# Where the early quarters of the first team's gate weights stand in SyncE's queue: between the attention loads or between the retention loads

## The reference, cut to what matters

```
h = rms_norm(x, g_mix)
proj = h @ w_in                      # q, k, v of 3 attention groups; retention q, k, v, g; two branch gates
outs, lses = per group (window, dilation): dilated_window_attention(q, k, v)       # 8 heads of 64
o_attn = sum over groups of softmax(lses) * outs
yr = retention_chunkwise(qr, kr, vr)                                               # 4 heads
o_ret = silu(gr_swish) * group_norm(yr)
merged = sigmoid(gate_a) * (o_attn @ w_attn_branch) + sigmoid(gate_r) * (o_ret @ w_ret_branch)
x = x + merged @ w_out
h2 = rms_norm(x, g_ffn)
y = hier_moe(h2, ...)                # 32 experts in 4 groups: top 1 group, top 2 experts inside it
out = rms_norm(x + y, g_final)
```

## Time and profile before

| | us |
|---|---|
| median of 3 runs | 804.96 |
| lowest, highest | 804.38, 806.15 |
| the profiled execution, its own time | 804.96 |
| its span | 803.2 |
| PE busy | 588.0 (73%) |
| DVE busy, ACT busy | 249.7, 196.9 |

### The profile page before, as it was taken

The page is one execution under the profiler, slowest core; times in us unless marked ns, Lnnn a source line. Parts: engine busy times, 40 slices in busy tenths (PEclk is TensorE's granted clock), DMA queues, the critical chain, the costliest instruction groups (busy, mean ns, idle before and its releaser), DMA issues.

```text
span 803.2 us, 11626 instructions
## 1 busy us (share of the span) xinstructions
PE 588.0 (73%) x4469; PEld 419.7 (52%) x4469; DVE 249.7 (31%) x432; ACT 196.9 (25%) x290; POOL 13.5 (2%) x28
## 2 busy tenths in 40 slices
PE   3999999999999999965690780780770870960966
PEld 3999999999999998852320320320320320320321
DVE  6776675866664455571000010010010010010001
ACT  5454554565555443330000000000000000000001
POOL 3000000000000000010000000000000000000000
PEclk9999999999999999988795795795895795895887
DMA  8758658255686555899999999999999999999991
GB/s 235 236 141 261 174 166 261 78 158 157 167 241 194 185 182 187 338 401 408 428 427 426 428 428 426 425 431 423 428 428 426 431 426 423 432 429 423 431 397 54
DMA packets 92758, 255.82 MB, mean 318 GB/s; under 512 B 8640, under 2 KB 70080, under 8 KB 80448
## 3 DMA queue, kind: packets, MB, share of 16 engines
q1 hardware_dynamic: 90512, 255.35, 82.9%
q10 hardware_dynamic: 2224, 0.17, 0.2%
HBM read 254.45 MB, written 1.05 MB: 318 GB/s over the span
## 4 chain that ended last, share of the span: by engine, by line
PE 65%; DMA 30%; DVE 2%; ACT 1%; issue 1%; POOL 0%; SPq 0%; DVEq 0%; ACTq 0%
PE ps L1032 64%; DMA ring<-in_w_down 27%; DMA ring<-in_w_up 2%; DMA gain<-in_g_mix 1%; ACT work L581 1%; DVE hn L706 1%; DVE work L887 0%; PE ps L1111 0%; POOL rstd L488 0%; PE ps L1135 0%; DVE hn L1026 0%; ACT work L673 0%; DVE hT L714 0%; DVE split L682 0%; DVE work L890 0%
## 5 line engine op out<-in xcount | busy, mean ns | idle before, releaser
L1032 PE MATMUL ps<-store,work 128*32 128x512 f32 x128 | 73.6, 740 | 182.2 <-DMA ring<-in_w_down 182.2
L1032 PE MATMUL ps<-ring,work 128*32 128x512 f32 x896 | 186.4, 614 | 1.6 <-DVE work L964 0.9
L682 DVE TENSOR_TENSOR split<-ring,split 128x768 fp32r<-128x768 f32 (+2 forms) x132 | 120.8, 932 | 92.4 <-ACT split L533 91.8
L1032 PE MATMUL ps<-hT,split 128*128 128x256 f32 x1152 | 141.9, 286 | 1.8 <-DVE hT L714 1.8
L1032 PEld LDWEIGHTS ps<-hT,split 128*128 128x128 f32 x1152 | 140.3, 194 | 2.8 <-issue 2.3
L1032 PEld LDWEIGHTS ps<-store,work 128*32 128x32 f32 x128 | 16.1, 132 | 232.1 <-DMA ring<-in_w_down 168.7
L533 ACT ACTIVATE split<-ring 128x768 fp32r<-128x768 f32 (+2 forms) x132 | 107.3, 825 | 120.2 <-PE ps L1032 101.6
L1032 PE MATMUL ps<-split,hT 128*128 128x256 f32 (+2 forms) x672 | 106.5, 316 | 0.0
L1032 PEld LDWEIGHTS ps<-split,hT 128*128 128x128 f32 x672 | 98.1, 190 | 4.4 <-issue 0.5
L964 DVE COPY work<-ps 128x512 f32<-128x512 f32 x8 | 5.5, 692 | 254.6 <-PE ps L1032 254.6
L1032 PE MATMUL ps<-hT_slot,work 128*32 128x512 f32 x128 | 73.6, 740 | 0.0
(11 more groups left out here) (176 smaller groups left out, 474.8 us busy)
## 6 DMA issues: line engine op xcount, KB each, us to landing
ring<-in_w_up SPq DMA_DIRECT2D x24, 2048.0 KB, 34.7
ring<-in_w_gate SPq DMA_DIRECT2D x18, 2048.0 KB, 24.9
ring<-in_w_in SPq DMA_DIRECT2D x96, 192.0 KB, 3.9
oRT_slot<-in_w_down SPq DMA_DIRECT2D x8, 2048.0 KB, 26.2
mid<-in_w_up SPq DMA_DIRECT2D x8, 2048.0 KB, 34.3
store<-in_w_down SPq DMA_DIRECT2D x8, 2048.0 KB, 17.4
hT_slot<-in_w_down SPq DMA_DIRECT2D x8, 2048.0 KB, 21.8
ring<-in_w_in SPq DMA_DIRECT2D x96, 128.0 KB, 2.4
```

Source lines behind the costliest of these rows:

```text
L682: dve.tensor_tensor(split[:, s, 1, 0:n], raw(s, n), split[:, s, 0, 0:n].bitcast(F32), ALU.subtract).then_inc(lo_ready, 1)
L1032: return pe.matmul(o, lhsT=l, rhs=r, start=start, stop=stop, skip_group_check=shared)
```

## The change

The sixteen quarters move from the attention loads to the retention loads. There are four retention iterations, as there were four attention iterations, so each iteration again takes quarter `i` of each of the four experts: one after the first quad, one after the second, two after the third. `load_pair` issues its three quads back to back. PE's wait for `early` names RET_HEADS in place of PAIRS, which is the same number. No other engine's stream changes.

```diff
-            def quarter(slot, src, i):
-                sp.dma_start(slots[slot][:, bass.ds(i * 1024, 1024)], src).then_inc(early, 16)
-
             def load_pair(i):
-                load_quad(3 * i, columns_of(attn_v[0], NG, P, i))
-                quarter(3, wg_v[0][:, bass.ds(i * 1024, 1024)], i)
-                load_quad(3 * i + 1, columns_of(attn_v[1], NG, P, i))
-                quarter(4, wg_v[1][:, bass.ds(i * 1024, 1024)], i)
-                load_quad(3 * i + 2, columns_of(attn_v[2], NG, P, i))
-                quarter(5, wg_v[2][:, bass.ds(i * 1024, 1024)], i)
-                quarter(10, wg_v[3][:, bass.ds(i * 1024, 1024)], i)
+                for m in range(3):
+                    load_quad(3 * i + m, columns_of(attn_v[m], NG, P, i))
 
             load_pair(0)
             with sp.Fori(1, PAIRS) as i:
                 load_pair(i)
 
+            def quarter(slot, src, i):
+                sp.dma_start(slots[slot][:, bass.ds(i * 1024, 1024)], src).then_inc(early, 16)
+
             with sp.Fori(0, RET_HEADS) as i:
                 load_quad(Q_RET + 3 * i, columns_of(qk_v, 2, RK, i))
+                quarter(3, wg_v[0][:, bass.ds(i * 1024, 1024)], i)
                 load_quad(Q_RET + 1 + 3 * i, plain_columns(COL_RV, RV, i))
+                quarter(4, wg_v[1][:, bass.ds(i * 1024, 1024)], i)
                 load_quad(Q_RET + 2 + 3 * i, plain_columns(COL_RG, RV, i))
+                quarter(5, wg_v[2][:, bass.ds(i * 1024, 1024)], i)
+                quarter(10, wg_v[3][:, bass.ds(i * 1024, 1024)], i)
...
-                    pe.wait_ge(early, 16 * TEAM * PAIRS)
+                    pe.wait_ge(early, 16 * TEAM * RET_HEADS)
```

## The result

| | kernel before | changed kernel |
|---|---|---|
| median of 6 runs, us | 804.57 | 810.79 |
| lowest to highest, us | 804.38 to 806.15 | 809.15 to 812.18 |
| ratio, 95% interval | | 1.0065, 1.0050 to 1.0081 |
| span of the profiled execution, us | 803.2 | 811.1 |

The median lies 2.8 us above the range. The ratio is that of the means, 810.09 us over 19 runs of the changed kernel (the table's six and thirteen more, 807.26 to 811.62 us) and 804.84 us over the six of the kernel before: 5.2 us. The two medians of the table are 6.2 us apart. Stretches of the changed kernel show where it went. The first row is an attention iteration, the next four are the retention iterations (each from PE's first matmul of one head to that of the next); the columns are those of the earlier trace rows.

What follows compares the result with a forecast made beforehand. PE's matmuls bound the kernel to 338.9 us, then the expert weights' DMA. Attention 0, retention 0 (0 to 0.2 at the dear end) and stream 0 left the time at 805.0 us, range 803.4 to 808.0.

Steps and rivals of the forecast that it cites:

- What bounds the kernel now: PE's own matmuls up to 338.9 us, then the expert weights' DMA; PE waits for no load in attention or retention.
- Attention gives nothing back: Attention stage: removing four 512 KB quarters an iteration gains 0, within bounds of 0 to 1.5 us.
- SP and throughput are not the bound: Retention iteration: SP busy 16.1 of 19.6 us; DMA 16.1 to 19.8 us, expected share 0.80 to 0.90.
- The first pair: Two quarters between quads 14 and 15 hold the queue up to 4.3 us; PE keeps 0.4 to 2.3 us of cover.
- the walk: Following quad 15's chunks behind the pair: chunk 3's low part ends at 179.5 us, PE wants it about 179.9 to 180.0.
- The tightest place: Quad 15 in the second retention iteration: 0.4 us left before PE at the dearest pair price, 2.3 at the cheapest.
- The single quarters: In retention, each delays loads behind it by 1.2 to 2.2 us and leaves PE at least 2 us.
- I don't expect the delays to add up: Between retention iterations no delay carries over, since DMA has time to spare and ScalarE's next wait is for PE.
- its own price for four quarters: DMA time that four quarters add to a retention iteration: 4.9 to 8.6 us.
- Rival (a): Retention: the pair makes PE wait through late low parts; 4.2 us, 809 us, at most 813 us; chance 0.09.
- The page of the Trainium skill: Weighed rule, 2 us plus bytes at 436 GB/s: 3.2 us a quarter, 6.4 us a pair; prediction held the trace disagrees.
- The sum that the prediction gave beside it, 3 us more: Total under the skill page's transfer prices: that of rival (a), some 3 us more.

Runs made afterwards that it cites:

- issues alone: Kernel before, with sixteen tiny DMAs added in retention where the changed kernel has its quarters, next to no bytes moved: 804.33 us, ratio 1.0003.
- second profile of the changed kernel: The changed kernel run once more, unaltered, next to the kernel before: 809.82 us, ratio 1.0066; the profiled execution took 812.93 us.

## Why the prediction was wrong, point by point

**What bounds the kernel now: right.** PE up to the stream, no wait on a load in either stage. **Attention gives nothing back: right** (34.30 us in both, at a share of 0.50). **SP and throughput are not the bound: right** (issues alone cost nothing; the forecast share of 0.80 to 0.90 was 0.79 to 0.86, and 0.91 was reached without loss).

**The first pair: right in one execution, and not in the other.** In the first profile the walk holds nearly to the tenth. The chunk load ahead of it lands at 165.67 + 2.5 = 168.2, the two quarters at 166.24 + 3.8 = 170.0 and 167.08 + 5.3 = 172.4 (issue by issue: KB, us to landing):

```profile
ring<-in_w_in SPq DMA_DIRECT2D x1, 128.0 KB, 2.5
...
ring<-in_w_gate SPq DMA_DIRECT2D x1, 512.0 KB, 3.8
...
spare<-in_w_gate SPq DMA_DIRECT2D x1, 512.0 KB, 5.3
```

A hold of 4.2 us, against 4.3 taken. Chunk 3 of quad 15, for which the walk gave 179.5 us, has its low part at

```profile
179.47 0.69 DVE L681 TENSOR_TENSOR split<-ring,split 128x512 fp32r<-128x512 f32 x1
```

that is 180.16, in a stage that began 0.57 us later, so at 179.6 by the prediction's clock. PE took it 0.28 us later. The tightest place was the right one. But 0.4 us of cover is less than the difference between executions: in the second profile of the changed kernel PE waited at this very chunk.

```profile
181.34 1.71 PE L1031 MATMUL ps<-hT,split 128*128 128x256 f32 x12 [0.97 <-DVE split L681]
```

So that the first profile shows no wait here was luck in part.

**The single quarters: the step that was missing.** The prediction said that they "by the same walk leave PE at least 2 us". It did not walk them. Chunk 0 of quad 17, the first behind a single quarter after the first pair, was ready at 187.35 + 0.69 = 188.04 and PE took it at 188.63: 0.6 us. The walk had started from the leads of the kernel before, and these were gone.

**"I don't expect the delays to add up": this step failed.** Its two reasons were that the DMA has time to spare and that ScalarE waits for PE again. The first was true and did not matter: a landing place waits for one low part, and the next load is issued only then, so the engines stand idle while the delay is handed on. The second was taken from the kernel before; in the changed kernel ScalarE waited for loads nine times in one iteration, and PE then waited for low parts, 5.0 us in all, where the prediction had 0 to 0.2. What recovers the lead is not the engines' spare time but PE's 19.64 us less the sum of a head's three loops. From numbers that the prediction had (1.1 us of issues, 2.4 to 2.8 us to land, 0.63 and 0.69) that is about 4.6 us a head, and its own price for four quarters was 4.9 to 8.6 us. The comparison that decided the case was made with the engines' 19.6 us instead. That attention loses nothing was no support either: the prediction speaks of two pairs in flight every 34 us, but an attention iteration has one pair and two singles in 34.3 us, and a retention iteration would have the same in 19.6.

**Rival (a) was the outcome, at 0.09.** Its mechanism (low parts late behind a pair) and its price (809 us) are close to 810.8. Its threshold was wrong: it does not decide from 4.7 to 5 us a pair. The four pairs held the queue for 4.2, 4.7, 5.2 and 4.4 us, and behind the last one, of 4.4 us, PE had its longest wait, 1.9 us (at the first chunk of the gates). The experiments set the condition: without the pair, or with three quarters, or with every other iteration free, nothing is lost. The range ended at 808.0 because a carry was excluded, and it was excluded by an argument, not by a row.

**The page of the Trainium skill.** The fit of the Trainium skill (SBUF — State Buffer) stands in the section "The DMA setup-cost knee", not in the one that the prediction names, and the page itself says that it overstates the cost at mid sizes. With nothing overlapped it gives the prediction's estimate of 6.4 us for a pair, and the trace of the changed kernel, with holds of 4.2 to 5.2 us, is below that as the one of before was. The sum that the prediction gave beside it, 3 us more, came nearer to the result than the forecast, by way of the wrong price.

## What to carry to other kernels

Where a buffer is refilled only once it is free, the question for an added transfer is not whether the DMA engines have time or whether one delay fits into the lead: add up the whole loop of the buffer (wait, issue, landing, each engine that works on it) over one round of the pattern, with the added transfers, and set it against the time of the engine that bounds the round. Well below that time delays vanish; above it, once the lead is used up, they cost their whole excess in every round, at a DMA share of 0.8 as well. The sum by parts is good to a microsecond or two here, not better. Close to the limit small things decide: a round left free or more landing places took the loss away, one issue less a chunk took most of it, and a pair taken apart two thirds.

## What was not expected of the hardware

Two quarters issued one behind the other land 2.4 to 2.7 us apart (170.0 and 172.4; later 191.3 and 193.9, 213.1 and 215.8), while a quarter is 1.2 us by bytes at the streaming rate of 428 GB/s. Chunk loads issued behind the pair are in flight in the same time (one from 168.72 to 173.1), so this is not the price of a quarter alone.

Waits of PE may cost more than their length. In the second profile of the changed kernel the granted clock of the gate quads is 0.96 in the mean (last row of its stretches above), and these quads took 48.10 us instead of 46.5. The fall comes right behind the retention stage, whose waits of PE for low parts are (total us, times, longest; then the stretches before and at the fall)

```profile
PE ps L1031 <- DVE split L681: 4.7, 4, 2.2
```

```profile
238.00:241.70 3.70, 1.46 (x14) 1.26 (x12) 1.23 (x1) 1.93 (x2) 0.00 (x0) 1.00 1.00 330
242.00:246.00 4.00, 4.00 (x23) 4.00 (x22) 3.42 (x8) 2.50 (x3) 1.56 (x1) 0.57 0.68 205
```

PE was busy for 1.46 of the 3.70 us ahead of the fall. 0.57 over 4 us is a time at each level, 1.2 and 2.4 GHz. In the first profile, with waits of 1.9 us at most, they took 46.7 us and the clock stayed at 2.4 GHz. That the waits brought the fall is likely by its place, but it was seen once and not tested.
